# Decode's key pages multiplied by the query on GpSimd instead of VectorE

## The chip, the cores and the metric

The kernel runs on one core of a Trainium2 chip. Its engines work side by side, each through its own list of instructions in order, and wait for one another by semaphores: TensorE (PE; its weight loads are PEld), VectorE (DVE), ScalarE (ACT), GpSimd (POOL), and SyncE (SP), which here only issues transfers. The metric is the device time of one execution in microseconds (us); before the change it is 2912.16 us, the median of 3 runs (2911.34 to 2912.66).

## The reference, cut to what matters

One inference step of a two-layer decoder for two groups that share the weights: a prompt of 1024 tokens, and 8 decode sequences with one new token each and 256 past tokens. The first layer is a gated linear recurrence, the second is differential attention over one shared key and value set, with 4 heads of two halves of 128. A decode sequence's past keys and values lie in 2 pages of 128 tokens, found by a page table. What the change touches is the first product below, for the past keys alone:

```
k_past = cache_k[page_table].reshape(nb, -1, DA_HEADS, 2 * DA_HEAD_DIM)
s = concatenate([einsum('bqhcd,bkhcd->bhcqk', q, k_past), einsum('bqhcd,bkhcd->bhcqk', q, k_new)], -1) * scale
s = s + rel_bias;  p = softmax(s);  a = p[:, :, 0] - lam * p[:, :, 1]
o = einsum('bhqk,bkhv->bqhv', a, v)
```

## The kernel before, in words

All weights come in slabs of 1 MB through one staging buffer, `w_stage`. SyncE issues a slab's two loads once the slab before it is split (it waits for `w_split`); GpSimd splits each into a high and a low part, `w_hi` and `w_lo`, with four instructions of 512 columns each (`split`, L657 and L661); TensorE multiplies with both parts. GpSimd does little else in the second layer. It takes the slabs strictly in their order, and of each it also waits until TensorE has left the slot (`w_used`). Slab `S_WOB` is the first of six of the output projection behind the attention.

The prompt's attention runs over 32 items, 4 heads with 8 query blocks each. VectorE does for each item the logits (L2093, L2095), their maximum (L2099), the weights after ScalarE's exponentials (L2107 to L2113) and a copy of the rows (L2122), between TensorE's scores, transposes and products with the values. In the last head decode's scores for the past keys are put in among these items. For each of the 8 sequences, SyncE loads two key pages of 128 tokens by 1024 columns into one pair of buffers, `k_page0` and `k_page1`, and the query, spread over all partitions, into one of two buffers `d_q_all`. The pages' addresses come from the page table by a register load (L545), the loads are L546, the query's is L550.

`page_scores(b)` on VectorE waits for pages and query, multiplies page 1 in place and signals ScalarE (`d_products`), multiplies page 0 in place (both L2165), and sums page 0 over each half head (L2169), which signals `pg_scored`. ScalarE sums page 1 with eight accumulating copies (`d_half`, L1648) and signals `d_halves`. SyncE waits for `pg_scored` before it loads the next page 0, and for `d_halves` before the next page 1. Two tables set where in the last head these steps stand: `SCORES_MID` puts sequences 0, 3 and 6 in the middle of items 1, 3 and 5, and `SCORES_END` puts 1, 2, 4, 5 and 7 at the ends of items 1 to 5; ScalarE's half follows the same tables. Behind sequence 5's pages and sequence 6's query SyncE's list has the loads of slab `S_WOB + 1`, and behind sequence 7's those of `S_WOB + 2`. Behind sequence 7 on VectorE comes `d_prepare` (L2147 to L2156), small copies and products for decode's bias and its own token.

Of the kernel before, what the change touches and what calls it, by code (L numbers as in the profile page):

```python
# [29 lines left out]
ALU = mybir.AluOpType  # L30
# [8 lines left out]
DEC = 8  # L39
# [41 lines left out]
def build(nc, i, o):  # L81
    ctx = ExitStack()
    with ctx:
# [4 lines left out]
        def at(name, shape, dt, offset):  # L88
            return nc.alloc_sbuf_tensor_at(name, shape, dt, offset=offset)
# [53 lines left out]
        def sem(name):  # L143
            return ctx.enter_context(nc.semaphore(name))
# [122 lines left out]
        d_products = sem("d_products")  # L267
        d_product = sem("d_product")
        dq_copied = sem("dq_copied")
        dq_stored = sem("dq_stored")  # L270
        dq_in = [sem(f"dq_in{s}") for s in range(2)]
# [6 lines left out]
        k_page_in = sem("k_page_in")  # L278
# [21 lines left out]
        def vec(n):  # L300
            return CT[:, 8 * n:8 * n + 8]
# [14 lines left out]
        S_KV, S_WOB, S_F1 = S_Q + 4, S_Q + 12, S_Q + 18  # L316
# [58 lines left out]
        KPG = [at(f"k_page{g}", [P, D], F32, arena + g * 4096) for g in range(NPG)]  # L375
        QBC = [at(f"d_q_all{s}", [P, D], F32, arena + 8192 + s * 4096) for s in range(2)]
# [47 lines left out]
        def nth(ph):  # L424
            return NORMS.index(ph)
# [4 lines left out]
        def hi_before(ph):  # L430
            return C * SCALINGS.index(ph)
# [170 lines left out]
        def _(pool):  # L602
# [8 lines left out]
            g = nc.gpsimd  # L611
# [7 lines left out]
            for l, bs in enumerate(LEVELS):  # L619

                half, n = bs // 2, P // bs
                v = lmask[l][:].rearrange("p (n h) -> p n h", h=half)
# [11 lines left out]
            def split(n, cols=SLAB, gain=None):  # L634


                s = n % 2
                hi, lo = (WHX[n - S_WOB - 4], WLX[n - S_WOB - 4]) if S_WOB + 4 <= n < S_F1 else (WH[s], WL[s])
                if n == 1:
                    pool.wait_ge(operand_split, C)  # L640
                if n in (S_F0 + 1, S_Q + 1, S_F1 + 1):
                    pool.wait_ge(operand_split, hi_before("ffn0" if n < S_Q else "kv" if n < S_F1 else "ffn1") + C)
                if n == S_Q + 1:
                    pool.wait_ge(norm_acc, (nth("kv") + 1) * (C - 1))
                pool.wait_ge(w_staged, n * 32 + 32)
                if gain is not None:
                    w3 = WST[:].rearrange("p (k n) -> p k n", k=C)
                    for u in range(4):
                        last = g.tensor_tensor(w3[:, 2 * u:2 * u + 2, :], w3[:, 2 * u:2 * u + 2, :],
                                               vec(gain)[:, 2 * u:2 * u + 2].unsqueeze(2).to_broadcast([P, 2, 256]), ALU.mult)  # L650
                    last.then_inc(w_scaled, 1)
                    pool.wait_ge(w_scaled, n - S_Q + 1)
                pool.wait_ge(w_used, n + 1)
                quarter = cols // 4
                parts = [slice(u * quarter, (u + 1) * quarter) for u in range(4)]
                for part in parts:
                    last = g.tensor_tensor(hi[:, part], WST[:, part], ones[:, 0:1].to_broadcast([P, quarter]), ALU.mult)  # L657
                last.then_inc(w_hi, 1)
                pool.wait_ge(w_hi, n + 1)
                for part in parts:  # L660
                    last = g.tensor_tensor(lo[:, part], WST[:, part], hi[:, part], ALU.subtract)  # L661
                last.then_inc(w_split, 1)
# [21 lines left out]
                    split(2 * h + 4, SLAB if 2 * h + 4 < S_WOA else EARLY * 256)  # L684
            for n in range(S_WOA + 1, S_WOA + 4):
                split(n, EARLY * 256)
            for n in range(S_WOA + 4, NSLAB):
                split(n, gain=G_MIX1 if S_Q <= n < S_KV else G_KV if S_KV <= n < S_WOB else None)


# [1071 lines left out]
        def _(dve):  # L1762
            v = nc.vector
# [376 lines left out]
            def rows(ap, c):  # L2140

                return ap.rearrange("p (h c) b -> p c h b", c=2)[:, c]
# [16 lines left out]

            def page_scores(b):  # L2160

                dve.wait_ge(k_page_in, 32 * (b + 1))
                dve.wait_ge(dq_in[b % 2], 16 * (b // 2 + 1))
                for g in (1, 0):
                    last = v.tensor_tensor(KPG[g][:], KPG[g][:], QBC[b % 2][:], ALU.mult)  # L2165
                    last.then_inc(d_products if g else d_product, 1)
                dve.wait_ge(d_product, b + 1)
                dst = STS[:, 0, :].rearrange("p (c h b) -> p h c b", c=2, h=AH)[:, :, :, b]
                v.tensor_reduce(dst, KPG[0][:].rearrange("p (h c n) -> p h c n", h=AH, c=2), AX, ALU.add).then_inc(pg_scored, 1)  # L2169
# [5 lines left out]
            for item in range(AH * NB):  # L2175
                h, n = item // NB, item % NB
                if item + 1 < AH * NB:
                    at_logit(item + 1)
                for g in fills(FILL_A, h, n):
                    kv_take(g)  # L2180
                if item:
                    at_rows(item - 1)
                if h and n == 0:
                    at_variance(h)
                if h == AH - 1 and n in SCORES_MID:
                    page_scores(SCORES_MID[n])
                if item + 1 < AH * NB:
                    at_weights(item + 1)
                for g in fills(FILL_B, h, n):
                    kv_take(g)  # L2190
                if 0 < n < NB - 1:
                    for m in rows_a(h, n + 1) + rows_b(h, n + 1):
                        at_scale((h - 1) * NB + m)
                if item == AH * NB - 2:
                    at_variance(AH, slice(0, EARLY_ROWS))
                    for c in range(3):
                        wob_rest(c)
                if h == AH - 1 and n in SCORES_END:
                    page_scores(SCORES_END[n])
                if h == AH - 1 and n == 5:  # L2200
                    d_prepare()
# [24 lines left out]
            def wob_add(w):  # L2226

                _, m, t = WOB_TILES[w]
                cols = rows_tile(t)
                dve.wait_ge(wob_full, w + 1)  # L2230
                dve.wait_ge(chunk_in[m], 48 if m < C - 1 else 32)
                v.tensor_tensor(X[:, m, cols], X[:, m, cols], PS[:, w % 3, 0:cols.stop - cols.start], ALU.add).then_inc(wob_free, 1)
# [24 lines left out]
            for c in range(2):  # L2257
                last = v.tensor_tensor(rows(DT1[:], c), rows(VSF[:], c), own, ALU.mult)
# [14 lines left out]
            for c in range(2):  # L2273
                last = v.scalar_tensor_tensor(out=rows(DG[:], c), in0=rows(DO[:], c), scalar=lam[:, 4 + c:5 + c],
                                              in1=DRS[:], op0=ALU.mult, op1=ALU.mult)
# [57 lines left out]
```

## Time and profile before

| what | value |
| --- | --- |
| median of 3 runs | 2912.16 us |
| the profiled execution | 2915.39 us, its span 2913.7 us |
| TensorE busy | 2795.3 us (96%) |
| VectorE busy | 1233.8 us (42%) |
| GpSimd busy | 1071.7 us (37%) |
| ScalarE busy | 575.0 us (20%) |
| chain that ended last | PE 88%, DVE 7%, ACT 2%, DMA 1% |

The shares are means over stages that differ. The change lies in one stage of some 120 us, from 1896 to 2017 us of the span, between the last head's first item and its last rows; there TensorE is busy for 80.16 us, VectorE for 80.03, ScalarE for 62.41 and GpSimd for 19.92. A row that names a tile, as `k_page<-k_page,d_q_all`, says what is written and what is read. An idle time in brackets is that of the engine before the row's first instruction, with what ended it.

### The profile page before, as it was taken

To read this page: it belongs to the slowest core of one execution; us is meant where nothing else is said; L and a number is where in the kernel's file an instruction comes from. 1 tells how busy PE (TensorE), PEld (TensorE's weight loads), DVE (VectorE), ACT (ScalarE), POOL (GpSimd) and SP (SyncE) were. 2 spreads that over 40 slices of the span, in tenths; PEclk is the share of its full clock that TensorE was granted. 3 is DMA by queue.
4 is the path that set the end of the run, shared out by engine and by line. 5 is a ranking of instruction groups with operands and counts; after the bars stand their busy time and mean duration, and the time that the engine had idled before them with its cause. 6 is when DMAs were issued, how large, how long until landed. Compare 5 with 4: busy or idle time off the path is not lost.

```text
span 2913.7 us, 43407 instructions
## 1 busy us (share of the span) xinstructions
PE 2795.3 (96%) x17625; PEld 2707.6 (93%) x17625; DVE 1233.8 (42%) x2149; ACT 575.0 (20%) x1160; POOL 1071.7 (37%) x938
## 2 busy tenths in 40 slices
PE   7999999989999999999999999976999999999998
PEld 6999999989999999999999888765899999999998
DVE  5344444443433333333351444556443333333335
ACT  3222222222300000000020233345130000000003
POOL 4333333324433443334436312311534433344331
PEclk8999999989999999999999999988999999999999
DMA  3211111121111111111131111145221111111111
GB/s 102 59 52 53 52 52 52 45 85 48 47 49 44 44 44 58 45 44 44 48 107 47 57 40 52 48 154 185 103 58 44 44 58 44 44 44 45 57 44 59
DMA packets 202239, 175.04 MB, mean 60 GB/s; under 512 B 6290, under 2 KB 185093, under 8 KB 202062
## 3 DMA queue, kind: packets, MB, share of 16 engines
q1 hardware_dynamic: 161728, 138.49, 15.3%
q10 hardware_dynamic: 40334, 33.95, 3.6%
q8 instruction: 140, 2.29, 0.3%
q14 instruction: 37, 0.30, 0.0%
HBM read 147.06 MB, written 25.36 MB: 59 GB/s over the span
## 4 chain that ended last, share of the span: by engine, by line
PE 88%; DVE 7%; ACT 2%; DMA 1%; issue 1%; POOL 1%; SPq 0%; ACTq 0%; PEld 0%; DVEq 0%; PEldq 0%; POOLq 0%
PE ps L698 25%; PE ps L700 25%; PE ps L699 25%; PE ps L888 3%; PE ps L1112 2%; PE ps L1132 1%; DVE rstd L1828 1%; DMA k_page<-in_cache_k 1%; DVE k_page L2165 1%; DVE stats L2099 1%; DVE act_lo L1833 1%; ACT probs L1593 1%; DVE probs L2093 1%; PE ps L1220 0%; PE ps L930 0%
## 5 line engine op out<-in xcount | busy, mean ns | idle before, releaser
L698 PE MATMUL ps<-act_hi,w_hi 128*128 128x344 f32 (+2 forms) x3808 | 1245.5, 327 | 24.1 <-DVE act_lo L1805 6.4
L699 PE MATMUL ps<-act_lo,w_hi 128*128 128x344 f32 (+2 forms) x3808 | 1223.2, 321 | 0.0
L700 PE MATMUL ps<-act_hi,w_lo 128*128 128x344 f32 (+2 forms) x3808 | 1222.9, 321 | 0.0
L657 POOL TENSOR_TENSOR w_hi<-w_stage,ones 128x512 fp32r<-128x512 f32 (+1 forms) x412 | 426.3, 1066 | 1376.8 <-PEq L748 1279.7
L698 PEld LDWEIGHTS ps<-act_hi,w_hi 128*128 128x128 f32 x3808 | 721.3, 189 | 38.8 <-issue 30.0
L699 PEld LDWEIGHTS ps<-act_lo,w_hi 128*128 128x128 f32 x3808 | 721.2, 189 | 3.5 <-issue 1.7
L700 PEld LDWEIGHTS ps<-act_hi,w_lo 128*128 128x128 f32 x3808 | 720.9, 189 | 0.0
L661 POOL TENSOR_TENSOR w_lo<-w_stage,w_hi 128x512 fp32r<-128x512 f32 (+1 forms) x412 | 535.9, 1333 | 8.1
L2013 DVE TENSOR_TENSOR resid<-resid,ps 128x344 f32<-128x344 f32 x528 | 270.0, 513 | 189.3 <-PE ps L700 188.9
L698 PE MATMUL ps<-h_hi,w_hi 128*128 128x344 f32 x1056 | 339.5, 321 | 2.7 <-DVE resid L2013 2.5
L700 PE MATMUL ps<-h_hi,w_lo 128*128 128x344 f32 x1056 | 337.2, 319 | 0.0
L699 PE MATMUL ps<-h_lo,w_hi 128*128 128x344 f32 x1056 | 337.1, 319 | 0.0
L1990 DVE TENSOR_TENSOR ps<-ps,rstd 128x344 f32<-128x344 f32 x132 | 68.9, 525 | 391.5 <-PE ps L700 391.5
L1993 DVE TENSOR_TENSOR ps<-ps,rstd 128x344 f32<-128x344 f32 x132 | 69.2, 525 | 363.2 <-PE ps L700 363.2
L1526 ACT ACTIVATE silu_gate<-ps 128x344 f32<-128x344 f32 x132 | 60.5, 459 | 810.0 <-DVE ps L1990 810.0
L698 PEld LDWEIGHTS ps<-h_hi,w_hi 128*128 128x128 f32 x1056 | 198.4, 188 | 5.8 <-DVE resid L2013 5.5
L700 PEld LDWEIGHTS ps<-h_hi,w_lo 128*128 128x128 f32 x1056 | 198.7, 188 | 0.0
L699 PEld LDWEIGHTS ps<-h_lo,w_hi 128*128 128x128 f32 x1056 | 198.6, 188 | 0.0
L1531 ACT CAST h_hi<-ps 128x344 fp32r<-128x344 f32 x132 | 59.0, 447 | 445.8 <-DVE ps L1996 445.8
L888 PEld LDWEIGHTS ps<-hg_q,hg_k 128*128 128x128 f32 x896 | 111.3, 198 | 5.4 <-DVE hg_k L1898 5.4
L888 PE MATMUL ps<-hg_q,hg_k 128*128 128x64 f32 x896 | 110.8, 278 | 4.9 <-DVE hg_k L1898 4.9
L674 POOL TENSOR_TENSOR state_sample<-state_sample,hg_f 128x1024 f32<-128x1024 f32 x8 | 15.6, 1946 | 234.6 <-DMA state_sample<-in_state_hgrn 234.6
(287 smaller groups left out, 2213.8 us busy)
## 6 DMA issues: line engine op xcount, KB each, us to landing
w_stage<-in_w_gate_up SPq DMA_DIRECT2D x88, 512.0 KB, 4.6
w_stage<-in_w_down SPq DMA_DIRECT2D x44, 512.0 KB, 4.1
w_stage<-in_w_in_a SPq DMA_DIRECT2D x32, 512.0 KB, 5.2
w_stage<-in_w_kv SPq DMA_DIRECT2D x16, 512.0 KB, 4.2
k_page<-in_cache_k SPq DMA_DIRECT2D x16, 512.0 KB, 4.1
v_page<-in_cache_v SPq DMA_DIRECT2D x16, 512.0 KB, 6.1
w_stage<-in_w_out_b SPq DMA_DIRECT2D x12, 512.0 KB, 4.6
x_spill<-resid ACTq DMA_DIRECT2D x8, 516.0 KB, 2.8
```

The source lines that it names most:

```text
L657: last = g.tensor_tensor(hi[:, part], WST[:, part], ones[:, 0:1].to_broadcast([P, quarter]), ALU.mult)
L661: last = g.tensor_tensor(lo[:, part], WST[:, part], hi[:, part], ALU.subtract)
L698: pe.matmul(out, wh, xh, start=first, stop=False)
L699: pe.matmul(out, wh, xl, start=False, stop=False)
L700: return pe.matmul(out, wl, xh, start=False, stop=last)
L888: last = pe.matmul(PS[:, 3 + l % 2, c * 64:(c + 1) * 64], K[h % 2][:, c * P:(c + 1) * P], q[:, c, :, 1, :], start=True, stop=True)
L1112: last = pe.matmul(PS[:, bank + k0 // 512, 0:k1 - k0], QA[:, 2 * h + c, n * P:(n + 1) * P], KTB[h % 2][:, c, k0:k1], start=True, stop=True)
L1526: a.activation(SIL[:, tile(t)], PS[:, t, 0:TS], ACT.Silu).then_inc(ffn_silu, 1)
L1531: a.copy(HH[par][:, k, tile(t)], PS[:, 3 + t, 0:TS]).then_inc(ffn_hh, 1)
L1990: v.tensor_tensor(PS[:, t, 0:TS], PS[:, t, 0:TS], RS[:, tile(t)], ALU.mult).then_inc(ffn_gscaled, 1)
L1993: v.tensor_tensor(PS[:, 3 + t, 0:TS], PS[:, 3 + t, 0:TS], RS[:, tile(t)], ALU.mult).then_inc(ffn_uscaled, 1)
L2013: v.tensor_tensor(X[:, m, tile(t)], X[:, m, tile(t)], PS[:, 6 + q % 2, 0:TS], ALU.add).then_inc(ffn_down_free, 1)
```

## The change

The 16 multiplications of the key pages leave VectorE. GpSimd does them by half pages, 512 columns each, page 1 first and then page 0, with the same waits for pages and query and the same two signals. They stand in GpSimd's list in two lots: sequences 0 to 5 ahead of the split of slab `S_WOB`, sequences 6 and 7 ahead of that of `S_WOB + 1`. VectorE keeps the sum of page 0 and its place in the list, ScalarE the sum of page 1.

```diff
--- before.py
+++ after.py
@@ -684,7 +684,23 @@
                     split(2 * h + 4, SLAB if 2 * h + 4 < S_WOA else EARLY * 256)
             for n in range(S_WOA + 1, S_WOA + 4):
                 split(n, EARLY * 256)
+            def page_products(b):
+
+                pool.wait_ge(k_page_in, 32 * (b + 1))
+                pool.wait_ge(dq_in[b % 2], 16 * (b // 2 + 1))
+                for pg in (1, 0):
+                    for u in range(2):
+                        half = slice(512 * u, 512 * (u + 1))
+                        last = g.tensor_tensor(KPG[pg][:, half], KPG[pg][:, half], QBC[b % 2][:, half], ALU.mult)
+                    last.then_inc(d_products if pg else d_product, 1)
+
             for n in range(S_WOA + 4, NSLAB):
+                if n == S_WOB:
+                    for b in range(6):
+                        page_products(b)
+                elif n == S_WOB + 1:
+                    for b in range(6, DEC):
+                        page_products(b)
                 split(n, gain=G_MIX1 if S_Q <= n < S_KV else G_KV if S_KV <= n < S_WOB else None)
 
 
@@ -2159,11 +2175,6 @@
 
             def page_scores(b):
 
-                dve.wait_ge(k_page_in, 32 * (b + 1))
-                dve.wait_ge(dq_in[b % 2], 16 * (b // 2 + 1))
-                for g in (1, 0):
-                    last = v.tensor_tensor(KPG[g][:], KPG[g][:], QBC[b % 2][:], ALU.mult)
-                    last.then_inc(d_products if g else d_product, 1)
                 dve.wait_ge(d_product, b + 1)
                 dst = STS[:, 0, :].rearrange("p (c h b) -> p h c b", c=2, h=AH)[:, :, :, b]
                 v.tensor_reduce(dst, KPG[0][:].rearrange("p (h c n) -> p h c n", h=AH, c=2), AX, ALU.add).then_inc(pg_scored, 1)
```

On GpSimd, from the pages of sequence 5 to the split of slab `S_WOB + 1` (`w_hi_55` and `w_lo_57` are the first slot of the split weights, `w_hi_56` and `w_lo_58` the second; `k_page_135` is page 1, `k_page_134` page 0, `d_q_all_136` and `137` the two query buffers), the difference is this, with + for what is there now; the two splits are those of slabs `S_WOB` and `S_WOB + 1`:

```order
+L694 TENSOR_TENSOR k_page_135<-k_page_135,d_q_all_137 128x512 x2
+L694 TENSOR_TENSOR k_page_134<-k_page_134,d_q_all_137 128x512 x2
+L657 TENSOR_TENSOR w_hi_55<-w_stage,ones 128x512 x4
+L661 TENSOR_TENSOR w_lo_57<-w_stage,w_hi_55 128x512 x4
+L694 TENSOR_TENSOR k_page_135<-k_page_135,d_q_all_136 128x512 x2
+L694 TENSOR_TENSOR k_page_134<-k_page_134,d_q_all_136 128x512 x2
+L694 TENSOR_TENSOR k_page_135<-k_page_135,d_q_all_137 128x512 x2
+L694 TENSOR_TENSOR k_page_134<-k_page_134,d_q_all_137 128x512 x2
 L657 TENSOR_TENSOR w_hi_56<-w_stage,ones 128x512 x4
 L661 TENSOR_TENSOR w_lo_58<-w_stage,w_hi_56 128x512 x4
```

Two pages' worth of products now stands between the two splits, and sequence 5's (with 0 to 4 above it) ahead of the first one.

On VectorE, the list around sequences 6 and 7 was this before:

```order
L2122 COPY q_all<-ps 128x2x128 [waits at_av_full]
L2165 TENSOR_TENSOR k_page_135<-k_page_135,d_q_all_136 128x1024 [waits dq_in0,k_page_in]
L2165 TENSOR_TENSOR k_page_134<-k_page_134,d_q_all_136 128x1024
L2169 TENSOR_REDUCE d_scores_tok<-k_page_134 128x4x2 [waits d_product]
L2107 RECIPROCAL stats<-stats 128x1 [waits at_exp]
L2108 TENSOR_SCALAR eps_s_squared<-stats 128x1
L2110 TENSOR_SCALAR stats<-stats,lam 128x1 [waits at_small]
L2113 SCALAR_TENSOR_TENSOR probs<-probs,stats 128x896 [waits at_small]
L2165 TENSOR_TENSOR k_page_135<-k_page_135,d_q_all_137 128x1024 [waits dq_in1,k_page_in]
L2165 TENSOR_TENSOR k_page_134<-k_page_134,d_q_all_137 128x1024
L2169 TENSOR_REDUCE d_scores_tok<-k_page_134 128x4x2 [waits d_product]
```

and is now this (line numbers have moved: the sum, L2169, is L2180 now):

```order
L2138 COPY q_all<-ps 128x2x128 [waits at_av_full]
L2180 TENSOR_REDUCE d_scores_tok<-k_page_134 128x4x2 [waits d_product]
L2123 RECIPROCAL stats<-stats 128x1 [waits at_exp]
L2124 TENSOR_SCALAR eps_s_squared<-stats 128x1
L2126 TENSOR_SCALAR stats<-stats,lam 128x1 [waits at_small]
L2129 SCALAR_TENSOR_TENSOR probs<-probs,stats 128x896 [waits at_small]
L2180 TENSOR_REDUCE d_scores_tok<-k_page_134 128x4x2 [waits d_product]
```

The two products of each sequence are gone; the sum stands where it stood and waits for the signal of page 0's product alone.

SyncE's list is the same before and after. Between the pages of sequences 5 and 6 it reads:

```order
L550 DMA d_q_all_136<-q_sample_rows 128x1024
L469 DMA w_stage<-in_w_out_b 128x4x256 [waits w_split]
L469 DMA w_stage<-in_w_out_b 128x4x256
L545 TENSOR_LOAD page_ids [waits pg_scored]
L545 ISA x2
L546 ISA
L546 DMA k_page_134<-in_cache_k 128x1024
L545 TENSOR_LOAD page_ids [waits d_halves]
```

The slab's loads wait for the split of slab `S_WOB`, and the page of sequence 6 stands behind them.

## Rows read from the trace of the kernel before

**Rows 1.** what VectorE waited for, 1896 to 2017 us: total, times, longest

```profile
DVE k_page L2165 <- DMA k_page<-in_cache_k: 21.6, 5, 6.0
```

**Rows 2.** VectorE in order of time: start, busy, line, operation, idle before and releaser

```profile
1908.22 2.35 DVE L2165 TENSOR_TENSOR k_page<-k_page,d_q_all 128x1024 f32<-128x1024 f32 x2
...
1918.31 2.36 DVE L2165 TENSOR_TENSOR k_page<-k_page,d_q_all 128x1024 f32<-128x1024 f32 x2 [4.46 <-DMA k_page<-in_cache_k]
...
1932.69 2.35 DVE L2165 TENSOR_TENSOR k_page<-k_page,d_q_all 128x1024 f32<-128x1024 f32 x2
...
1943.14 3.23 DVE L2165 TENSOR_TENSOR k_page<-k_page,d_q_all 128x1024 f32<-128x1024 f32 x2 [3.00 <-DMA k_page<-in_cache_k]
...
1955.48 2.36 DVE L2165 TENSOR_TENSOR k_page<-k_page,d_q_all 128x1024 f32<-128x1024 f32 x2 [6.03 <-DMA k_page<-in_cache_k]
...
1966.72 2.35 DVE L2165 TENSOR_TENSOR k_page<-k_page,d_q_all 128x1024 f32<-128x1024 f32 x2
...
1977.44 4.26 DVE L2165 TENSOR_TENSOR k_page<-k_page,d_q_all 128x1024 f32<-128x1024 f32 x2 [2.61 <-DMA k_page<-in_cache_k]
...
1990.08 2.36 DVE L2165 TENSOR_TENSOR k_page<-k_page,d_q_all 128x1024 f32<-128x1024 f32 x2 [5.56 <-DMA k_page<-in_cache_k]
1992.48 1.22 DVE L2169 TENSOR_REDUCE d_scores_tok<-k_page 128x8 f32<-128x1024 f32 x1
```

**Rows 3.** the chain of waits after page 3, and after page 7

```profile
1947.65 0.27 SPq L545
...
1949.45 6.01 DMA k_page<-in_cache_k
...
2003.12 6.23 PE ps L1132 x14
```

**Rows 4.** GpSimd's groups by shape, whole span: busy, mean ns of one, idle before

```profile
L661 POOL TENSOR_TENSOR w_lo<-w_stage,w_hi 128x512 fp32r<-128x512 f32 x396 | 519.4, 1344 | 7.8
...
L668 POOL TENSOR_TENSOR hg_o<-hg_o,hg_gate 128x1032 f32<-128x1032 f32 x7 | 16.6, 2370 | 51.9 <-DVE hg_o L1871 51.9
```

**Rows 5.** GpSimd in order of time, around the pages

```profile
1935.10 4.04 POOL L657 TENSOR_TENSOR w_hi<-w_stage,ones 128x512 fp32r<-128x512 f32 x4 [74.95 <-PEq L748]
1939.22 4.94 POOL L661 TENSOR_TENSOR w_lo<-w_stage,w_hi 128x512 fp32r<-128x512 f32 x4
1971.81 4.04 POOL L657 TENSOR_TENSOR w_hi<-w_stage,ones 128x512 fp32r<-128x512 f32 x4 [27.66 <-DMA w_stage<-in_w_out_b]
```

**Rows 6.** SyncE's DMA issues in order of time

```profile
1898.46 1.48 SPq L546 DMA_DIRECT2D k_page<-in_cache_k  x2
...
1962.30 0.98 SPq L469 DMA_DIRECT2D w_stage<-in_w_out_b  x2
1971.05 1.48 SPq L546 DMA_DIRECT2D k_page<-in_cache_k  x2
...
1983.68 1.76 SPq L546 DMA_DIRECT2D k_page<-in_cache_k  x2
1985.49 0.98 SPq L469 DMA_DIRECT2D w_stage<-in_w_out_b  x2
```

**Rows 7.** DMA issues of the page: count, KB each, median us to landing

```profile
k_page<-in_cache_k SPq DMA_DIRECT2D x16, 512.0 KB, 4.1
```

**Rows 8.** ScalarE's additions of a key page: ns min/median/max

```profile
L1648 ACT ACTIVATE k_page<-k_page x64: 292/293/311, 1909.5 to 1993.4; 128x128 f32<-128x128 f32 x64
```

**Rows 9.** engines busy, granted clock, DMA share and GB/s in one stretch

```profile
1983.60:1992.10 8.50, 2.97 (x13) 2.09 (x11) 2.94 (x3) 2.61 (x7) 0.00 (x0) 0.79 0.81 246
```

**Rows 10.** VectorE with GpSimd idle, and the last with it busy

```profile
1993.95 0.26 DVE L2150 COPY d_rel_rows<-d_rel 33x32 f32<-33x32 f32 x2
...
1994.42 0.29 DVE L2156 TENSOR_TENSOR d_prod<-q_sample,k_sample 128x32 f32<-128x32 f32 x2
...
2031.28 1.14 DVE L2216 TENSOR_SCALAR v_page<-v_page,d_a_sum 128x256 f32<-128x256 f32 x4
...
2045.97 4.54 DVE L2216 TENSOR_SCALAR v_page<-v_page,d_a_sum 128x256 f32<-128x256 f32 x4
```


## The prediction

> **What bounds the kernel now.** I read the waits of VectorE in the stretch of the page products first. Between 1896 and 2017 us its longest wait is for key pages: five times, 21.6 us in all [rows 1]. Then I read VectorE in order of time: eight pairs of products, in the text pages 0 to 7, one pair for each sequence. Where a row shows an idle time released by the DMA, VectorE had nothing else that it could do in its order; pages 1, 3, 4, 6 and 7 are of this kind, while pages 0, 2 and 5 were there before VectorE came to them [rows 2]. Third, the chain of waits: after page 3 it runs from VectorE's sum to SyncE's table read, to the page's DMA, and back to VectorE's product [rows 2, 3]. So these pages are no background work. One pair of buffers is loaded, multiplied, summed and loaded again, and the attention items of the last head wait between them in VectorE's order.
>
> The end of a sum is the start of the pair of products, its duration, a step of 0.03 and the sum's 1.22. For page 0 this is 1908.22 + 2.35 + 0.03 + 1.22 = 1911.82, for page 7 1993.70: 81.9 us for seven turns [rows 2]. From a sum's end to the next product, where VectorE waits for the page, are 6.49, 6.84, 7.86, 7.12 and 7.12 us (pages 1, 3, 4, 6, 7), mean 7.09. I call that the load gap: SyncE's reads and issues and the two transfers.
>
> **Part 1: the products change engine.** VectorE loses 16 instructions, two a page, 2.36 us a page undisturbed. GpSimd gets 32, four a page. It multiplies elsewhere in the same form, two full inputs in SBUF, in place: 2370 ns for 1032 columns, or 1.18 us for 512, so 4.70 a page; with three steps between instructions 4.74 [rows 4]. The bounds are 4 x 1.01 = 4.04, the row with one broadcast input [rows 5], and 4 x 1.344 = 5.38, the mean of the subtraction, which includes its disturbed instances [rows 4]. I take 4.74, since operation and operands are the same.
>
> The sum of the new turn, where load and product are waited for: 7.09 + 4.74 + 0.05 for the signal + 1.22 = 13.10 us. What the move gains is that GpSimd starts when the page lands, not when VectorE's order reaches it. That helps pages 0, 2 and 5. The two loads of page 0 are issued from 1898.46 on within 1.48 us, and one lands a median 4.1 after its issue [rows 6, 7]: I take 1903.7. Its product ends at 1908.4, about when VectorE arrives (1908.22), and its sum ends at 1909.7 instead of 1911.82, 2.1 earlier.
>
> Five turns of 13.10 then put the sum of page 5 at 1909.7 + 65.5 = 1975.2. In between I looked whether VectorE's other work is later than the page. For page 2 it arrives at 1932.69 plus the 0.9 by which page 1 is late, 1933.6, while the product ends at 1934.6. For page 5 it needs 7.63 us after the sum of page 4 (1959.09 to 1966.72), thus 1969.7, while the product ends at 1973.9. Both times it waits. Before, the sum of page 5 ended at 1970.32: 4.9 later.
>
> ScalarE's sum starts half-way through the product, and its 8 x 0.293 = 2.34 us [rows 8] run beside the other 2.4 of the product and VectorE's sum; I cost it at nothing. Wholly uncovered, it would hold the next load of that buffer by those 2.34 less the sum's 1.22, 1.1 us a page.
>
> **Part 2: GpSimd's order.** The split of the first slab of the output projection ran at 1935.10, while VectorE did the pages, and took 4.04 + 0.08 + 4.94 = 9.06 us [rows 5]. Now it stands behind the product of page 5. SyncE has the next slab's two loads directly ahead of page 6's, and they wait until that split is done (before, they were issued at 1962.30, long before page 6 at 1971.05 [rows 6]). So page 6 is no longer released by VectorE's sum alone: product end 1973.9 + 0.1 + 9.06 = 1983.1, and only then SyncE issues the slab, 1 MB, and behind it page 6, 1 MB. The row for such a pair is page 7 with the slab behind it: issued from 1983.68 on, and moved by about 1992.1, at 246 GB/s [rows 6, 9]. That is 8.5 us for 2 MB; here page 6 is the last of the two, so it lands at 1991.6. Bounds: 7.09 if the page were not held up by the slab, 10 if the later issues added their 1.5. Product, signal and sum: 1997.6, against 1982.96, 14.6 later. This turn takes 22.4 us instead of 13.1; the split's place alone costs 9.3.
>
> Page 7 follows by one common turn: 2010.7, against 1993.70. Check: 6 x 13.1 + 22.4 = 101.0 against 81.9, less the 2.1 won at the start, is 17.0 us.
>
> **Part 3: behind page 7.** The second slab's split ran from 1971.81 on, beside page 6 [rows 5]. Now it starts 0.1 us after the last product and lasts 9 us, beside VectorE's small preparation of the decode bias. VectorE's scaling of the value pages took 1.14 us for four with GpSimd idle and 4.54 with GpSimd splitting, 0.85 more for each [rows 10]. Four of the preparation's instructions, two copies and two multiplications, read SBUF only (0.26 and 0.29 a pair [rows 10]). Bounds are 0 and 4 x 1.24 = 5.0, a whole GpSimd instruction each; I take 2.5, as three of the four waiting 0.85, since they are far smaller than that row's. Nothing covers it: the next logits stand behind them in VectorE's order. The logits read PSUM and I cost their disturbance at nothing.
>
> The Trainium skill, "SBUF — State Buffer", section Who interferes with whom, says that VectorE with two SBUF inputs and GpSimd reading SBUF exclude each other for a whole instruction, and that the later one blocks. By that rule the two multiplications block fully and the copies only in a fast mode, 2.5 us for the two alone; the row agrees in kind.
>
> What was behind stays behind: after page 7 the chain goes through the last logits, the softmax and TensorE's weighted values at 2003.12 [rows 3], all in order, with no fixed date that could absorb a delay. So the whole 17.0 + 2.5 = 19.5 us come to the end.
>
> The Trainium skill, "GPSIMD Engine Reference", section 3.1 (Elementwise), speaks against the move: a two-input addition of 2048 columns took 4497 ns on GpSimd, 1.96 times VectorE's. An estimate from that page's figure is 4.5 us a page, and the total would be 17.6 instead of 19.5. This case's row is slower, and I keep it.
>
> **Sum.** The profiled execution took 2915.39 us, its span 2913.7. Its sum is 2915.4 + 19.5 = 2934.9; the median of the runs shown lies 3.2 lower, at 2912.16, so the forecast is 2931.7 us.
>
> **The rivals.**
> First, page 6 is not held: the split hides under VectorE's work, or the order lets the page go first. Then page 6 takes a common turn and the cost is 19.5 - 9.3 = 10.2, time 2922.4. For it: splits have mostly run in shadow. Against: the order shows the wait ahead of the page.
>
> Second, everything on the loop is disturbed: product 5.38, load gap 7.86 as at page 4, the turn 14.5, and 5.0 behind page 7. The sum with the same steps is 31.8, time 2944. For it: the product's neighbours on GpSimd do reach 5.38. Against: VectorE mostly waits while GpSimd multiplies, so there is little to collide with.
>
> Third, on the other side: GpSimd's early start outweighs its slowness, at the pages where VectorE came late (0, 2, 5). With product 2.36 as on VectorE and no hold of page 6 the same steps give page 7 at 1987.5, 6.2 earlier, time 2906.0. It decides from the point where the product is 17.0 - 9.3 = 7.7 us, over seven pages 1.1 each, shorter than 4.74: at 3.6 us a page. Against: no GpSimd row of this size is under 4.04, and the hold would have to go too.
>
> **Chances.** Forecast 0.70, with its own range of 14 to 26 us more (2926 to 2938, product 4.2 to 5.1 and the small terms); first rival 0.12; second 0.11; third 0.04; another way of no change 0.03. A difference under 0.2% (5.8 us) can't be told from none here. The third gives faster 0.04, the last same 0.03, the rest slower, 0.93. The range reaches to the first rival's middle and nearly to the second's: 2921 to 2943.
>
> **What would show it.** In the profile after: GpSimd's four products a page at 4.7 us in all; sums 13 us apart where they were 10 to 14; page 6's issue directly behind the first slab's split and a turn of about 22 us; page 7's sum about 17 us later; VectorE's wait in front of the sum, released by GpSimd, where it was in front of the product, released by the DMA. Wrong would be: page turns still near 11.7 on average, page 6 issued before the split's end, or the last sum later but the weighted values not.

## The result, and the profile after

The changed kernel took 2933.45 us (median of 4 runs, 2930.43 to 2936.06) against 2911.75 (4 runs of the kernel before): 21.7 us more; the ratio on record is 1.0077, with a 95% interval from 1.0065 to 1.0089. Ratios and intervals here and below stand beside the medians and can differ from the quotient of two medians by some 0.0004. The forecast was 2931.7, with a range of 2926 to 2938. The profiled execution took 2936.06 us, its span 2934.3, which is 20.6 longer than the span before. Lines below the diff have moved: products L694, VectorE's sum L2180, preparation L2166 and L2172, logits L2109, weighted values L1148.

The busy times of each engine over the whole span, to be set against the table of before:

```profile
PE 2794.8 (95%) x17625; PEld 2705.0 (92%) x17625; DVE 1214.1 (41%) x2133; ACT 574.7 (20%) x1160; POOL 1111.6 (38%) x970
```

VectorE has 19.7 us less work, GpSimd 39.9 more, and TensorE as much as before. VectorE's freed time went into waiting. The longest waits of VectorE and of GpSimd, 1896 to 2037 us (total, times, longest):

```profile
DVE d_scores_tok L2180 <- POOL k_page L694: 60.3, 8, 16.7
```

```profile
POOL k_page L694 <- DMA k_page<-in_cache_k: 102.6, 8, 44.0
```

Where VectorE waited 21.6 us for pages [rows 1] it now waits 60.3 for GpSimd's products, in front of every sum. GpSimd in turn waits for every page (the 44.0 is the idle time before page 0, which costs nothing). GpSimd in order of time:

```profile
1902.68 5.05 POOL L694 TENSOR_TENSOR k_page<-k_page,d_q_all 128x512 f32<-128x512 f32 x4 [44.02 <-DMA k_page<-in_cache_k]
1915.88 4.93 POOL L694 TENSOR_TENSOR k_page<-k_page,d_q_all 128x512 f32<-128x512 f32 x4 [8.14 <-DMA k_page<-in_cache_k]
...
1969.75 5.06 POOL L694 TENSOR_TENSOR k_page<-k_page,d_q_all 128x512 f32<-128x512 f32 x4 [8.48 <-DMA k_page<-in_cache_k]
1974.77 4.03 POOL L657 TENSOR_TENSOR w_hi<-w_stage,ones 128x512 fp32r<-128x512 f32 x4
1978.88 4.94 POOL L661 TENSOR_TENSOR w_lo<-w_stage,w_hi 128x512 fp32r<-128x512 f32 x4
1992.30 4.93 POOL L694 TENSOR_TENSOR k_page<-k_page,d_q_all 128x512 f32<-128x512 f32 x4 [8.48 <-DMA k_page<-in_cache_k]
2005.21 4.93 POOL L694 TENSOR_TENSOR k_page<-k_page,d_q_all 128x512 f32<-128x512 f32 x4 [7.97 <-DMA k_page<-in_cache_k]
2010.09 4.03 POOL L657 TENSOR_TENSOR w_hi<-w_stage,ones 128x512 fp32r<-128x512 f32 x4
```

Four products take 4.93 to 5.09 us; before, VectorE did the same page in 2.36 [rows 2]. The first slab's split, at 1935.10 before [rows 5], now stands at 1974.77, between pages 5 and 6. What SyncE does around it (DMA issues):

```profile
1896.96 1.48 SPq L546 DMA_DIRECT2D k_page<-in_cache_k  x2
...
1963.25 1.43 SPq L546 DMA_DIRECT2D k_page<-in_cache_k  x2
...
1983.85 0.94 SPq L469 DMA_DIRECT2D w_stage<-in_w_out_b  x2
1985.54 1.48 SPq L546 DMA_DIRECT2D k_page<-in_cache_k  x2
```

The next slab's loads, at 1962.30 before and so 8.75 us ahead of page 6 [rows 6], go out at 1983.85, 0.03 us after the split's end, and page 6 directly behind them. VectorE in order of time, the eight sums and what follows the last:

```profile
1907.77 1.22 DVE L2180 TENSOR_REDUCE d_scores_tok<-k_page 128x8 f32<-128x1024 f32 x1 [0.96 <-POOL k_page L694]
...
1920.84 1.22 DVE L2180 TENSOR_REDUCE d_scores_tok<-k_page 128x8 f32<-128x1024 f32 x1 [8.95 <-POOL k_page L694]
...
1934.37 1.22 DVE L2180 TENSOR_REDUCE d_scores_tok<-k_page 128x8 f32<-128x1024 f32 x1 [1.19 <-POOL k_page L694]
...
1948.07 1.22 DVE L2180 TENSOR_REDUCE d_scores_tok<-k_page 128x8 f32<-128x1024 f32 x1 [8.64 <-POOL k_page L694]
...
1961.30 1.22 DVE L2180 TENSOR_REDUCE d_scores_tok<-k_page 128x8 f32<-128x1024 f32 x1 [10.18 <-POOL k_page L694]
...
1974.84 1.22 DVE L2180 TENSOR_REDUCE d_scores_tok<-k_page 128x8 f32<-128x1024 f32 x1 [3.61 <-POOL k_page L694]
...
1997.27 1.22 DVE L2180 TENSOR_REDUCE d_scores_tok<-k_page 128x8 f32<-128x1024 f32 x1 [16.70 <-POOL k_page L694]
...
2010.17 1.22 DVE L2180 TENSOR_REDUCE d_scores_tok<-k_page 128x8 f32<-128x1024 f32 x1 [10.12 <-POOL k_page L694]
...
2011.64 1.51 DVE L2166 COPY d_rel_rows<-d_rel 33x32 f32<-33x32 f32 x2
...
2013.37 0.90 DVE L2172 TENSOR_TENSOR d_prod<-q_sample,k_sample 128x32 f32<-128x32 f32 x2
2014.19 1.80 DVE L2109 TENSOR_SCALAR probs<-ps,far_bias 128x1536 f32<-128x1536 f32 x1
```

Sums end 13.1, 13.5, 13.7, 13.2, 13.5, 22.4 and 12.9 us apart, 102.4 in all. The same seven turns took 10.1, 14.4, 11.3, 11.5, 11.2, 12.6 and 10.7 before (by the working on [rows 2]), 81.9. The chain of waits (start, us, what), ScalarE's sum of page 1 behind sequence 0, one turn, and the weighted values:

```profile
1907.76 2.36 ACT k_page L1664 x16
...
1920.84 1.23 DVE d_scores_tok L2180
1922.09 0.27 SPq L545
...
1923.88 5.29 DMA k_page<-in_cache_k
1929.24 1.26 POOL k_page L694
...
2022.68 5.84 PE ps L1148 x14
```

The loop is sum, table read, page, product, as before [rows 3], with GpSimd's product in VectorE's place. The weighted values start at 2022.68 instead of 2003.12, 19.56 later. That is: the turns +20.5; the way from page 0's issue to its sum -1.3 (12.03 us, 13.36 before); from the last sum to the logits +1.9 (2.80, 0.93 before); and this execution came to page 0's issue 1.5 us earlier, before any changed instruction had run. These add up to the 19.6. The remaining 1.0 of the span's 20.6 arose behind.

### The profile page after: what moved, and what is told of

Its sections match the earlier page's. It is cut to its first block, busy times and chain, and to the rows that moved or that the text cites. A ratio compares the mean times of both kernels' runs of the same rounds, so it can differ in the third digit from the quotient of the medians.

```text
span 2934.3 us, 43423 instructions
## 1 busy us (share of the span) xinstructions
PE 2794.8 (95%) x17625; PEld 2705.0 (92%) x17625; DVE 1214.1 (41%) x2133; ACT 574.7 (20%) x1160; POOL 1111.6 (38%) x970
## 3 DMA queue, kind: packets, MB, share of 16 engines
q1 hardware_dynamic: 161728, 138.49, 15.2%
## 4 chain that ended last, share of the span: by engine, by line
PE 87%; DVE 5%; POOL 2%; issue 2%; ACT 2%; DMA 2%; SPq 0%; ACTq 0%; PEld 0%; DVEq 0%; POOLq 0%; PEldq 0%
PE ps L714 25%; PE ps L716 25%; PE ps L715 25%; PE ps L904 3%; PE ps L1128 2%; PE ps L1148 1%; POOL k_page L694 1%; DVE rstd L1844 1%; DMA k_page<-in_cache_k 1%; DVE stats L2115 1%; DVE act_lo L1849 1%; ACT probs L1609 1%; POOL w_lo L661 1%; PE ps L1236 0%; PE ps L937 0%
```

## The experiments

The theory: the time is the loop's. Each turn costs load, product and sum in series, GpSimd's product is about 2.6 us longer than VectorE's, and the split between pages 5 and 6 holds one page for some 9 us more. The rivals: the hold costs nothing, the loss is the product alone; or the reverse; or a disturbance of VectorE makes it. Differences are to the kernel before on the same chip; "turns" are the seven of each run's one profile, 81.9 before and 102.4 after. Three kernels share one loop (the changed kernel, the same again, and the one with the preparation cleared, which differs only behind the turns), and their turns are 102.4, 103.2 and 104.6: two profiles of one loop can differ by 2 us. A numbered page is, as in the prediction, the pair of one sequence; where page 0 and page 1 of a pair are meant, the text says so.

**The hold alone.** The kernel before, VectorE multiplying, with one wait more on GpSimd.

```diff
                 if n == S_WOB:
+                    pool.wait_ge(pg_scored, 6 + OPENED)
```

> The kernel before, VectorE multiplying, with GpSimd's split of the first output slab waiting for the sum of page 5: the second part of the change alone. Loop theory: sum of page 5 at 1970.3, split 9.1, then slab and page 6 together 8.5, so page 6 lands at about 1988 instead of 1977.4; page 3's product is no longer disturbed (0.9 less): about 9.7 us more, 2921.5. Rival (the hold is hidden under VectorE's own work, as splits mostly are): within 2 us of the kernel before.

2920.63 us against 2909.8: ratio 1.0036 (1.0021 to 1.0051), +10.8 us. VectorE's product of page 6:

```profile
1982.74 3.20 DVE L2167 TENSOR_TENSOR k_page<-k_page,d_q_all 128x1024 f32<-128x1024 f32 x2 [11.78 <-DMA k_page<-in_cache_k]
```

Its turn took 22.3 us, 9.6 more than before, and the other six 3.4 less in all, so the turns came to 88.1. The hold costs by itself, with no product on GpSimd. The timed 10.8 is more than the turns' 6.3; the interval (6 to 15) reaches both.

**The hold taken out, in two ways.** First the split goes ahead of page 3:

```diff
-                    for b in range(6):
+                    for b in range(3):
...
-                    for b in range(6, DEC):
+                    for b in range(3, DEC):
```

> The changed kernel, with the split of the first output slab put ahead of the product of page 3 instead of behind that of page 5. Loop theory (the time is set by the one pair of page buffers: load gap 7.1, product 5.0, sum 1.2, and by SyncE's list holding page 6 until that split): page 6's turn falls from 22.4 to 13.4 us, the split ends about 1 us after page 3 has landed, so net 8 us less, about 2925.5, still 14 above the kernel before. Rival (sharing SBUF between GpSimd and VectorE is what costs): the same instructions run, as many beside VectorE's work, so no change, about 2933.

2925.75 against 2909.8: 1.0059 (1.0041 to 1.0077), +16.0. GpSimd in order of time:

```profile
1937.24 4.93 POOL L661 TENSOR_TENSOR w_lo<-w_stage,w_hi 128x512 fp32r<-128x512 f32 x4
1942.13 4.92 POOL L694 TENSOR_TENSOR k_page<-k_page,d_q_all 128x512 f32<-128x512 f32 x4
...
1980.97 4.94 POOL L694 TENSOR_TENSOR k_page<-k_page,d_q_all 128x512 f32<-128x512 f32 x4 [8.13 <-DMA k_page<-in_cache_k]
```

Page 6 follows page 5 in a common turn of 13.1, and the turns fall to 93.6, as expected. Page 3 has no idle time in front: it had landed, and stood behind the split; its turn became 15.2.

Then the split stays, and only SyncE's list changes: the slab's loads go behind page 7.

```diff
-                if b == 5:
-                    columns(S_WOB + 1, w_out_b, 256)
+            columns(S_WOB + 1, w_out_b, 256)
             columns(S_WOB + 2, w_out_b, 512)
```

> The changed kernel, with SyncE's loads of the second output slab moved from between pages 5 and 6 to behind page 7; GpSimd's list is the changed one, the split still between the products of pages 5 and 6. Loop theory: page 6 loads under the split, its product starts when the split ends, so its turn is 9.1 + 0.1 + 5.0 + 0.05 + 1.2 = 15.4 instead of 22.4, 7 us less, about 2926.5. Rival (the split's own time on GpSimd is the cost, not SyncE's wait): at most the 2 us by which a split exceeds a load gap change, so 2931 to 2933.

2925.61 against 2909.8: 1.0057 (1.0039 to 1.0075), +15.8; turns 93.0. GpSimd:

```profile
1977.29 4.94 POOL L660 TENSOR_TENSOR w_lo<-w_stage,w_hi 128x512 fp32r<-128x512 f32 x4
1982.18 4.95 POOL L693 TENSOR_TENSOR k_page<-k_page,d_q_all 128x512 f32<-128x512 f32 x4
```

The page's product follows the split at once. Page 6's turn was 13.9, not 15.4: that figure was counted from the product's end, not from the sum's, 1.3 us later. Both kernels agree: with the hold gone, some 16 us remain by the time (intervals from 11 to 22), and 11 to 12 in the turns. In the main they belong to the product; in the first kernel about 2 of them are page 3's wait behind the split.

**Half of the product.** GpSimd multiplies only the first half of each page; the other half's products are left out.

```diff
-                    for u in range(2):
+                    for u in range(1):
```

> The changed kernel with only the first half of each key page multiplied on GpSimd; the other half's products are left out. Product 2.5 instead of 5.0 us a page, all waits, loads and the order kept. Loop theory (product one for one on the loop): page 0 gains the 1 us that VectorE waited there, page 2 the 1.2 before VectorE's own work sets it, the six other turns 2.5 each: 16 to 17 us less than the changed kernel, some 5 above the kernel before. Rival (the signal between engines and the hold are the cost, not the multiplication): 5 us less at most.

2915.81 against 2910.94: 1.0019 (1.0010 to 1.0029), +4.9. The products by shape (ns min, median, max):

```profile
L694 POOL TENSOR_TENSOR k_page<-k_page,d_q_all x16: 1259/1266/1731, 1899.9 to 1988.1; 128x512 f32<-128x512 f32 x16
```

Turns 85.4, 17.0 less than with whole products; 7 turns of 2.45 us are 17.1. The time is where it was expected, some 5 above the kernel before. Each of the seven turns became 2.0 to 3.2 us shorter: a shorter product shortens every turn, and nothing else takes its place. GpSimd's half product (2.5 us) is nearly VectorE's whole one (2.36), and this kernel keeps the hold: set against the hold alone its turns are 2.7 us less (timed 4.9 more than before against 10.8, with intervals that overlap). That hints that starting when the page lands is worth something, as the third rival had it, but 2.7 us is hardly more than profiles of one loop differ, so it is not shown. The whole product is too long for it in any case.

**Page 0 first.** The order of the two pages of a pair in the product is turned round.

```diff
-                for pg in (1, 0):
+                for pg in (0, 1):
```

> The changed kernel, with page 0 multiplied before page 1. VectorE gets its page 2.5 us earlier at each sequence, ScalarE 2.5 later. Loop theory: the second load of each turn now waits for ScalarE's sum, 5.0 + 2.4 = 7.4 us after landing, about where it was issued before, so the turns stay at 13.4 within 0.5; only the last sum, behind which VectorE goes on, is 2.5 earlier: about 2931. Rival (VectorE's wait for its own page is the cost, not the loop): 2.5 us less at each of seven or eight pages, about 2914.

2925.99 against 2909.8: 1.0059 (1.0041 to 1.0077), +16.2; turns 95.1. The expectation was missed in part: the turns were to stay and fell by 7.3. SyncE's issues at page 2, and the time from issue to landing of all 16 page loads:

```profile
1916.71 4.01 SPq L546 DMA_DIRECT2D k_page<-in_cache_k  x2
```

```profile
DMA to landing us min/median/max: 3.3/3.5/6.0
```

VectorE's sum now runs beside the second half of the product, so the first load leaves early and the second 3.7 us behind it, when ScalarE is done. At pages 1, 2, 4, 5 and 7 the loads left 2.6 us or more apart, and each of these ten landed 3.3 to 3.8 us after its issue. In the changed kernel the two leave 1.1 us apart: at pages 1 to 5 the first lands after 3.4 to 3.6 us, as soon as one that is ahead alone, and the second after 5.0 to 5.6. (A median over all 16 mixes first and second loads: 4.5 in the changed kernel, but 3.7 in the kernel with the split ahead of page 3, whose loads also leave together.) Products start 11.6 to 12.1 us apart on the undisturbed pages. The query's load follows the second page at once in both kernels, so it does not make the difference. The load gap is therefore no constant: the second load pays when it is issued close behind the first.

**The changed kernel again, and the preparation cleared.** The second makes GpSimd's last split wait until VectorE's preparation is done.

```diff
                 elif n == S_WOB + 1:
                     for b in range(6, DEC):
                         page_products(b)
+                    pool.wait_ge(d_dve, D_DVE["prod"])
```

> The changed kernel, unchanged, beside the next three on one chip, so that they can be set against it. Every theory: 19 to 22 us above the kernel before on the same chip.

> The changed kernel, with the split of the second output slab waiting until VectorE's small preparation behind page 7 is done. Theory (GpSimd's split delays those small instructions): the preparation goes back from 2.75 us between the last sum and the logits to 0.9, the last split ends 2 us later where nobody waits for it; 1.9 us less than the changed kernel. Rival (their longer spans in the trace are not on the path): no change within 0.5 us, the logits starting as late as before.

The changed kernel: 2934.93 against 2910.92, 1.0082 (1.0069 to 1.0096), +24.0, turns 103.2; 19 to 22 had been expected, which the interval (20 to 28) reaches. Cleared: 2930.49, 1.0069 (1.0056 to 1.0083), +19.6, turns 104.6. VectorE behind the last sum, cleared:

```profile
2013.55 0.26 DVE L2167 COPY d_rel_rows<-d_rel 33x32 f32<-33x32 f32 x2
...
2014.01 0.30 DVE L2173 TENSOR_TENSOR d_prod<-q_sample,k_sample 128x32 f32<-128x32 f32 x2
```

Copies and products are back at 0.26 and 0.30, and from the sum to the logits it is 0.92 us instead of 2.80. The profile settles what the disturbance was and that it came from the split. The timed 4.4 us between the two is within overlapping intervals and no measure of the 1.9 expected.

**Versions with the pages loaded and awaited apart.** In all three SyncE loads page 1 of a pair first, as soon as ScalarE has summed it, and page 0 of the pair after VectorE's sum, and each of the two has its own semaphore:

```diff
-                if b:
-                    sp.wait_ge(pg_scored, b + OPENED)
-                page(kc, KPG[0], k_page_in, b, 0)
                 if b:
                     sp.wait_ge(d_halves, b)
-                page(kc, KPG[1], k_page_in, b, 1)
+                page(kc, KPG[1], k_page_in[1], b, 1)
+                if b:
+                    sp.wait_ge(pg_scored, b + OPENED)
+                page(kc, KPG[0], k_page_in[0], b, 0)
```

On GpSimd, with the split ahead of page 3 and a wait for each page of a pair in front of its products:

> GpSimd multiplies, the first output split stands ahead of page 3 as in the earlier run, and the two pages of a pair get signals of their own: SyncE loads page 1 as soon as ScalarE has summed it, then page 0 once VectorE has. Loop theory: the turn is that of page 1 alone, product 2.5 + ScalarE's sum 2.4 + issue 0.6 + one load 3.6 to 4.1 = 9.1 to 9.6 us where VectorE does not come later itself, against 13.4 in the changed kernel and 11.7 in the one before: over seven turns about 12 us less than before, 10 after the disturbed preparation, so 2900 where the kernel before takes 2910. Rival (GpSimd's speed limits it whatever the loads do): turns of 12 and more, no gain over the earlier run with the early split, about 14 above before.

2916.21 against 2910.92: 1.0021 (1.0012 to 1.0030), +5.3; turns 85.1. Its turns are 8.4 us less than with the pages awaited together and the split ahead of page 3 (93.6), but the time expected, some 2900, is missed. SyncE, and GpSimd at page 3:

```profile
1909.70 1.43 SPq L546 DMA_DIRECT2D k_page<-in_cache_k  x2
```

```profile
1936.86 4.93 POOL L661 TENSOR_TENSOR w_lo<-w_stage,w_hi 128x512 fp32r<-128x512 f32 x4
1941.74 4.93 POOL L694 TENSOR_TENSOR k_page<-k_page,d_q_all 128x512 f32<-128x512 f32 x4
```

VectorE had done the first sum by 1906.79 there, but SyncE's list had page 1 of the pair first and ScalarE came late, so both loads left 2.9 us later. Page 3 waited for the split again, in a turn of 16.4. And page 7's turn took 13.4: ScalarE's sum of page 6 began at 1978.8, behind attention work in its own list, though page 6's products had ended at 1977.3. The expected turn of 9.1 to 9.6 left out ScalarE's order; one turn of the seven was near it (9.65).

On VectorE, the rest as in the kernel before:

```diff
-                dve.wait_ge(k_page_in, 32 * (b + 1))
                 dve.wait_ge(dq_in[b % 2], 16 * (b // 2 + 1))
                 for g in (1, 0):
+                    dve.wait_ge(k_page_in[g], 16 * (b + 1))
```

> The kernel before, VectorE multiplying, with the two pages loaded and awaited apart in the same way. Loop theory: product 1.2 + ScalarE's sum 2.4 + issue 0.6 + load 4.1 = 8.3 us a turn where VectorE waits for the page (five of seven), against 10.1 to 12.6; the turns that VectorE's own work sets stay. About 8 to 10 us less than the kernel before, some 2901 where that takes 2910. Rival (the two loads share the transfer engines, so loading them apart gains nothing): no change within 2 us.

2906.21 us (11 runs) against 2910.92: 0.9985 (0.9976 to 0.9994), 4.7 us faster, where 8 to 10 had been expected; the interval runs from 1.7 to 7.0. Turns 74.5, 7.4 less than before. By this small margin it is faster than both kernels. VectorE's waits, its products at page 1, and SyncE's issues of page 2:

```profile
DVE k_page L2165 <- DMA k_page<-in_cache_k: 11.9, 8, 3.7
```

```profile
1913.46 1.22 DVE L2165 TENSOR_TENSOR k_page<-k_page,d_q_all 128x1024 f32<-128x1024 f32 x1 [2.67 <-DMA k_page<-in_cache_k]
1915.46 1.23 DVE L2165 TENSOR_TENSOR k_page<-k_page,d_q_all 128x1024 f32<-128x1024 f32 x1 [0.77 <-DMA k_page<-in_cache_k]
```

```profile
1917.88 1.44 SPq L546 DMA_DIRECT2D k_page<-in_cache_k  x2
```

The first of a pair is multiplied while the second travels, and the wait for pages falls from 21.6 [rows 1] to 11.9 us. The two loads do not leave further apart than before: SyncE waited for ScalarE in every turn, VectorE's sum was done by then, and two issues still take 1.4 us. What gained here is that the two are awaited apart, not that they travel apart.

Shared: of each pair GpSimd multiplies page 1 only and VectorE page 0, with the split ahead of the pair of sequence 3.

```diff
-                for pg in (1, 0):
+                for pg in (1,):
...
+                dve.wait_ge(dq_in[b % 2], 16 * (b // 2 + 1))
+                dve.wait_ge(k_page_in[0], 16 * (b + 1))
+                v.tensor_tensor(KPG[0][:], KPG[0][:], QBC[b % 2][:], ALU.mult).then_inc(d_product, 1)
```

> Pages loaded and awaited apart as in the two earlier runs; GpSimd multiplies page 1 alone, VectorE page 0, with the first output split ahead of page 3. If the two engines' products block each other, VectorE's product of page 0 takes 1.2 to 2.5 us where it meets GpSimd's 2.5; page 1's loop is 2.5 + ScalarE 2.4 + 0.6 + 3.6 to 4.1 = 9.1 to 9.6, the version with VectorE alone has 8.3. Loop theory: 0 to 6 us slower than that version, so about the kernel before, 2906 to 2912 where that takes 2911. Rival (sharing the multiplication between two engines relieves VectorE, whose order sets the turns): faster than VectorE alone, under 2904.

2913.22 against 2910.94: 1.0009 (1.0000 to 1.0018), +2.3; turns 78.4. That is just above the 2906 to 2912 expected, and not the better version. The split before page 3's product was in the way again: ScalarE summed that page late, and the next turn took 14.9. Where both engines multiply at once they meet; VectorE at page 6, against 1.23 at page 7:

```profile
1972.10 2.33 DVE L2180 TENSOR_TENSOR k_page<-k_page,d_q_all 128x1024 f32<-128x1024 f32 x1 [1.30 <-DMA k_page<-in_cache_k]
```

## Why the prediction was right, step by step

The mechanism was right: a loop in which GpSimd's longer product counts in every turn, and one page held behind a split. The two sizes that were off are the product and the start.

**The turn.** 13.10 was forecast; the five turns up to page 5 took 13.4 on average, page 7's 12.9. The load gap came out as forecast: from a sum's end to the product 7.10 us on average over the six common turns, 7.09 forecast. The product was under-sized: 4.74, measured 4.93 to 5.09. The tile's group shows one at 1.27 us, where 1.18 had been scaled down from 1032 columns:

```profile
L694 POOL TENSOR_TENSOR k_page<-k_page,d_q_all x32: 1260/1266/1338, 1902.7 to 2008.9; 128x512 f32<-128x512 f32 x32
```

Scaling by columns leaves out what an instruction may cost however short it is. A straight line through 512 columns in 1266 ns and 1032 in 2370 [rows 4] has 2.12 ns a column and about 0.18 us of fixed part. This is an estimate from two sizes; no run multiplied a page in fewer, longer instructions, so a fixed part is not shown to be the cause. The Trainium skill, "GPSIMD Engine Reference", section 3.1 (Elementwise), gives a figure for 2048 columns from which 4.5 us a page was estimated; the trace differs, with 4.93 and more, so this estimate was further off than the 4.74.

**The start.** From page 0's issue to its sum 11.25 was forecast (1898.46 to 1909.7) and 12.03 measured: the pages landed 0.5 later (the median of 4.1 [rows 7] mixes first and second loads; these took 4.3 and 4.5) and the product took 0.3 more. The gain over before was 1.3, not 2.1.

**Page 6.** Right in mechanism and size. The split followed page 5's product and took 9.05 us (9.06); from the slab's issue to the product 8.45 (8.5); the turn 22.4 (22.4). The hold alone raised that turn by 9.6, against 9.3 in the forecast, and either way of removing it brought the turn back to 13 or 14 us. The first rival, in which page 6 is not held, would have been 10.2 us; with the hold taken out 16 were timed, intervals from 11 to 22. Product and start cost some 2.2 of this difference, as in the changed kernel, and page 3's wait behind the split about 2 in one of the two kernels; the rest is not accounted for.

**Behind page 7.** 2.5 us forecast, 1.9 measured. The size was near, the division was not: the two copies grew by 1.25 (0.26 to 1.51), the two multiplications by 0.6 (0.29 to 0.90). The rule in the Trainium skill, "SBUF — State Buffer", section Who interferes with whom, names copies in a fast mode and instructions with two SBUF inputs as those that GpSimd can block for a whole instruction. The trace agrees in kind, and with the split held back the delays were gone. In size it does not bear out a whole instruction for each: of the pair of copies one waited about one GpSimd instruction, the two multiplications grew by 0.6 together where 2.5 had been worked out for them by that rule, and at 0.14 us the single copy between the pairs did not wait. Whether the copies ran in a fast mode no run here shows. The second rival's 5.0 did not come, nor its disturbed products: VectorE mostly waited while GpSimd multiplied.

**ScalarE's sum at nothing.** Behind page 0 it ended last (1907.76 and 2.36 us, to 1910.12 in the chain) and released the next load of page 1 in the chain, yet that turn took 13.1, no longer than the others. In the chain's next three turns VectorE's sum released the loads. So in this kernel ScalarE's sum was covered.

**The sum.** Turns +20.5 and start -1.3 make 19.2 where 17.0 were forecast: 1.4 from the product (six common turns, 80.0 us against 78.6) and 0.8 at the start. The preparation took 0.6 less, and 1.5 were won by an earlier arrival ahead of the changed instructions. That the weighted values came 19.56 us later, almost the 19.5 forecast, is therefore in part luck: 2.2 more and 2.1 less than forecast nearly cancel. Timed, the change cost 21.7 us (18.9 to 25.9 by the interval) against 19.5.

What stays open: the profiles' turns and the times differ by a few us in single kernels (the hold alone 6.3 and 10.8, this change 20.5 and 21.7 to 24.0), so that how the total divides between product (about 11 to 16) and hold (about 6 to 11) is known only to that.

## What to carry to other kernels

When work moves to an idle engine, ask first whether it lies on a loop with a buffer: if load, product and sum wait for one another, the slower engine's extra time counts in every turn, and the old engine's freed time turns into waiting. Look at what the new engine has behind the moved work in its list, and at whose queue waits for that: here a weight split behind page 5 held a page on SyncE, for 9 us. And in such a loop, let the parts be awaited apart: the kernel before with its two pages awaited apart gained 4.7 us (1.7 to 7.0), while moving the product lost 22. Letting them travel apart is worth trying too: only the kernel with page 0 first had loads that did in most turns, and its turns were 7.3 us less than the changed kernel's.

## What had not been expected of the hardware

Of two 512 KB loads issued 1.1 us apart the first landed 3.4 to 3.6 us after its issue and the second, the one that counts, after 5.0 to 5.6 (pages 1 to 5 of the changed kernel), while those issued 2.6 us or more apart took 3.3 to 3.8 each. GpSimd's time for half a page did not shrink in proportion: 1.27 us for 512 columns, 2.37 for 1032. And small instructions of VectorE can wait about as long as a GpSimd instruction takes. VectorE's scaling of the query rows after the change, with GpSimd idle, and beside page 2's product:

```profile
1911.28 0.61 DVE L2148 TENSOR_SCALAR q_all<-q_all,row_factor 128x256 f32<-128x256 f32 x2
...
1930.46 2.72 DVE L2148 TENSOR_SCALAR q_all<-q_all,row_factor 128x256 f32<-128x256 f32 x2
```

Here 2.1 us came on top for two instructions, beside GpSimd instructions of 1.27 us; VectorE's wait for the product, which followed, hid it.
